# A fp32 transformer layer on one core: the last weight transfers in parts, a branch and a spread moved, and one quarter of the residual added by the array

## The chip, the cores and the metric

The kernel runs on one core of one Trainium2 chip. The metric is the device time of one execution, in microseconds (us). The engines of a core run their own instruction streams and wait for each other by semaphores: TensorE (PE) multiplies, VectorE (DVE) and ScalarE (ACT) do elementwise work, SyncE (SP) issues most transfers, GpSimd (POOL) makes constants.

## What is computed

One layer on 256 tokens of width 1024, all in float32: a mixer (dilated sliding attention and an mLSTM, with an output projection, added to x) gives x1, and a mixture of 32 experts, 4 for each token, gives what is added to x1.

```python
h = rmsnorm(x, norm1_g)
...
x = x + jnp.einsum('bse,ed->bsd', mixed, w_out[l])        # x1
x = x + moe_ffn(rmsnorm(x, norm2_g[l]), w_router[l], ...)

# moe_ffn, for the tokens tok of one expert e
gu = jnp.dot(xb, w_gate_up[e]) + b_gate_up[e]             # 1024 x 2048
gate = jnp.minimum(gu[:, :D_FF], SWIGLU_LIMIT)
up = jnp.clip(gu[:, D_FF:], -SWIGLU_LIMIT, SWIGLU_LIMIT)
act = gate * jax.nn.sigmoid(SWIGLU_ALPHA * gate) * (up + 1.0)
return jnp.dot(act, w_down[e]) + b_down[e]                # 1024 x 1024
```

## The kernel before

**Weights.** Every expert has 12 MB of weights: its gate and up matrix as 4 pieces of 2 MB (256 rows each, gate pieces in what follows) and its down matrix as 2 pieces of 2 MB (512 rows each, down pieces). A ring of 12 pieces in SBUF holds them. SP issues one transfer for each piece in the order of `LOAD_ORDER`: expert after expert, but at the end the four gate pieces of expert 30, the four of expert 31, the two down pieces of 30, and the two of 31. Before each, SP waits until PE has used what stood in that place of the ring (`gu_used`, `d_used`). One partition takes 16 KB of a piece. Only the very last piece comes as two transfers of 1 MB, the second one on the semaphore `ld_last`.

**Slots.** An expert works on 64 slots (CAP). PE gathers its tokens from x1 (`xres`) by a product with a 0/1 matrix (`pick`), turns them, multiplies them with the gate pieces into banks 0 and 1, and DVE and ACT make the activation `up_c` of them. PE turns that (`turn_act`), multiplies with the down pieces into bank 6 (`down`, ACT copies the result to `y_sb`, L787), and adds y to the tokens by a product with the turned slots (`spread`, L1509) into four banks of PSUM that stay open over all experts: `ACC`, one for each half of 128 tokens (t) and half of the width (c). `y_sb` has room for one expert, so the spread of an expert must be through before ACT copies the next one's y.

**Order on PE.** For each expert: the bias (L1413), the gate pieces (L1548), the slots' transposes (L1559), the spread of the expert before (L1509), the gathering for the next (L1475), `turn_act` (L1568), `turn_rows` (L1486) and the down pieces (L1584). Experts 1 to 28 run in a hardware loop of two (its branch is L1632); expert 0, expert 29 and the last two are written out. In `last_two` the gate pieces of 31 come ahead of the down pieces of 30, and the spread of 30 stands between the two down pieces of 31.

**Overflow.** If an expert has more than 64 tokens, rounds over all experts follow in a branch. DVE sets `flag` early; each engine loads it and compares (`overflow`, L384). In this data the flag is 0 and the branch jumps over the rounds' code. On PE this stands behind the last down products (L1643), and the last spread behind it.

**End.** DVE adds x1 to each of the four banks (L1136), SP stores each quarter of the output, 256 KB, when its sum is there (L542), and waits for all four.

The first part of the kernel, the mixer, takes some 150 us; nothing in it changes but semaphores that are merged.

## Time and profile before

| | |
|---|---|
| median of 3 runs | 1058.16 us (1057.73 to 1058.27) |
| profiled execution, its own time | 1057.47 us |
| its span, first to last instruction | 1055.7 us |
| mean granted TensorE clock | 1.000 |
| PE busy | 1035.1 us, 98% of the span |
| DVE, ACT busy | 198.9 us, 141.8 us |
| read from HBM | 423.31 MB, 402 GB/s over the span |

The profiled execution took 1.8 us more than its span, which is what lies around the program, and 0.7 us less than the median of the runs. PE counts as busy while matmuls overlap in it, so 98% doesn't say that it is at its peak. A 512-column float32 product stands in the profile as two MATMUL rows (two passes); those of 64 columns of weights run two at a time beside each other, so that the 16 rows of a 2 MB piece take 3.6 us. What bounds a stretch is read from what ended the idle time ahead of it, in brackets.

### The profile page before, as it was taken

How to read it: one execution, taken by the hardware profiler on the slowest of the kernel's cores; microseconds unless marked ns; L12 is line 12 of the kernel's file. 1: busy time of each engine (PE TensorE's matmuls, PEld its weight loads, DVE VectorE, ACT ScalarE, POOL GpSimd, SP SyncE). 2: the span in 40 equal slices, each digit the busy share in tenths (PEclk: the TensorE clock that was granted, in tenths of full speed). 3: DMA queues.
4: the chain of work that ended last, by engine and by line, in shares of the span. 5: the costliest groups of instructions: out<-in, count | busy, mean ns of one | idle time of the engine just before them, and what ended most of it. 6: DMA issues, size and time to landing. Idle time of an engine off the chain costs nothing.

```text
span 1055.7 us, 11898 instructions
## 1 busy us (share of the span) xinstructions
PE 1035.1 (98%) x4771; PEld 385.3 (37%) x4771; DVE 198.9 (19%) x502; ACT 141.8 (13%) x297; POOL 5.5 (1%) x23
## 2 busy tenths in 40 slices
PE   9999999999999999999999999999999999999997
PEld 5655543333333333333333333333333333233332
DVE  2162232111111111111111111111111111101111
ACT  2144431101111110010011111111111011001101
POOL 1000000000000000000000000000000000000000
PEclk9999999999999999999999999999999999999999
DMA  9964699999999999999999999999999999999996
GB/s 336 366 231 160 264 372 398 430 427 429 430 427 429 428 428 428 428 429 428 428 428 428 428 428 430 428 429 428 429 428 428 429 429 429 428 428 429 427 428 253
DMA packets 40875, 424.63 MB, mean 402 GB/s; under 512 B 6384, under 2 KB 7448, under 8 KB 15640
## 3 DMA queue, kind: packets, MB, share of 16 engines
q1 hardware_dynamic: 40840, 424.37, 95.9%
q8 instruction: 13, 0.21, 0.1%
q14 instruction: 6, 0.05, 0.0%
q10 hardware_dynamic: 16, 0.00, 0.0%
HBM read 423.31 MB, written 1.05 MB: 402 GB/s over the span
## 4 chain that ended last, share of the span: by engine, by line
PE 79%; DMA 14%; SPq 6%; issue 0%; DVE 0%; another core or an unknown queue 0%; ACT 0%; POOL 0%; DVEq 0%; POOLq 0%
PE bank L1548 33%; PE bank L1584 17%; DMA ring<-in_w_gate_up 14%; PE bank L1166 7%; PE bank L1509 4%; PE bank L1475 4%; SPq L392 4%; PE bank L1360 3%; PE bank L1413 2%; PE bank L1486 2%; PE bank L1568 2%; SPq L401 1%; PE bank L1202 1%; PE bank L1559 1%; PE bank L1144 0%
## 5 line engine op out<-in xcount | busy, mean ns | idle before, releaser
L1548 PE MATMUL bank<-ring,xe_t 128*64 128x512 f32 x2048 | 450.0, 594 | 10.3 <-DMA ring<-in_w_gate_up 9.8
L1548 PEld LDWEIGHTS bank<-ring,xe_t 128*64 128x64 f32 x2048 | 142.8, 137 | 314.0 <-issue 289.3
L1584 PE MATMUL bank<-ring,late 128*64 128x512 f32 x992 | 219.9, 595 | 0.6 <-DMA ring<-in_w_down 0.6
L1584 PEld LDWEIGHTS bank<-ring,late 128*64 128x64 f32 x992 | 68.8, 137 | 127.6 <-issue 124.0
L1085 DVE TENSOR_SCALAR gate_c<-bank 128x512 f32<-128x512 f32 x32 | 22.1, 692 | 439.4 <-PE bank L1548 439.4
L771 ACT ACTIVATE s_sb<-bank 128x256 f32<-128x256 f32 x32 | 12.3, 383 | 460.3 <-PE bank L1559 460.3
L1166 PE MATMUL bank<-ring 128*128 128x512 f32 x160 | 72.0, 596 | 0.5 <-issue 0.5
L1509 PE MATMUL bank<-late,s_sb 64*128 64x512 f32 x256 | 63.6, 615 | 0.7 <-ACT late L787 0.7
L1475 PE MATMUL bank<-xres,pick 128*64 128x512 f32 x248 | 60.0, 605 | 0.0
L787 ACT ACTIVATE late<-bank 128x512 f32<-128x512 f32 x32 | 19.1, 597 | 229.2 <-PE bank L1584 229.2
L1083 DVE COPY row_of<-fold 128x64 f32 x31 | 6.0, 195 | 195.1 <-PE bank L1413 195.1
L1166 PEld LDWEIGHTS bank<-ring 128*128 128x128 f32 x160 | 29.1, 190 | 31.6 <-issue 31.3
L1067 DVE TENSOR_TENSOR xe_t<-bank,g_run 128x512 f32<-128x512 f32 (+1 forms) x33 | 22.2, 675 | 87.5 <-PE bank L1486 87.4
L1413 PE MATMUL bank<-bgu,row_of 32*64 32x512 f32 x256 | 34.8, 613 | 0.0
L1509 PEld LDWEIGHTS bank<-late,s_sb 64*128 64x128 f32 x256 | 22.0, 186 | 22.5 <-issue 20.9
L1475 PEld LDWEIGHTS bank<-xres,pick 128*64 128x64 f32 x248 | 15.0, 136 | 41.2 <-issue 41.2
L760 ACT ACTIVATE late<-bank 128x512 f32<-128x512 f32 x31 | 18.5, 597 | 85.9 <-PE bank L1475 85.9
L1360 PE MATMUL bank<-ring 128*128 128x512 f32 x64 | 28.3, 592 | 0.0
L1568 PEld LDWEIGHTS bank<-ident,up_c 128*128 128x128 f32 x128 | 17.9, 210 | 26.0 <-issue 25.1
L1568 PE MATMUL bank<-ident,up_c 128*128 128x128 f32 x128 | 24.0, 310 | 0.0
L1486 PE MATMUL bank<-ident,late 128*128 128x128 f32 x124 | 23.1, 309 | 0.6
L1089 DVE SCALAR_TENSOR_TENSOR up_c<-up_c,gate_c 128x512 f32<-128x512 f32 x32 | 22.2, 692 | 1.2
(207 smaller groups left out, 420.4 us busy)
## 6 DMA issues: line engine op xcount, KB each, us to landing
ring<-in_w_gate_up SPq DMA_DIRECT2D x126, 2048.0 KB, 35.7
ring<-in_w_down SPq DMA_DIRECT2D x62, 2048.0 KB, 33.9
ring<-in_w_in SPq DMA_DIRECT2D x5, 2048.0 KB, 15.0
ring<-in_w_out SPq DMA_DIRECT2D x2, 2048.0 KB, 10.4
ring<-in_w_gate_up SPq DMA_DIRECT2D x4, 1024.0 KB, 8.0
ring<-in_w_down SPq DMA_DIRECT2D x4, 1024.0 KB, 25.7
ring<-in_attn_bias SPq DMA_DIRECT2D x1, 1536.0 KB, 18.1
xres<-in_x SPq DMA_DIRECT2D x2, 512.0 KB, 4.8
```

The lines of the kernel that those rows point to most:

```text
L392: sp.dma_start(gu_half(s), w_gate_up[0, e, h * RUN * P:(h + 1) * RUN * P, :].rearrange("(p j) n -> p j n", j=RUN))\
L1067: return dve.tensor_tensor(xe_t.rearrange("p (c b) n -> p c b n", c=2)[:, :, lo:hi, :], bank[7][:, :].rearrange("p (b c n) -> p c b n", b= ...
L1089: dve.scalar_tensor_tensor(out=up_c, in0=up_c, scalar=1.0, in1=gate_c, op0=ALU.add, op1=ALU.mult).then_inc(act_half, 1)
L1166: mm = pe.matmul(dst[:, :], ht[:, k, t * P:(t + 1) * P], win[:, b % WINS, k, :], start=(k == 0), stop=(k == KD - 1))
L1360: mm = pe.matmul(bank[ACC[2 * t + c]][:, :], mix_t[:, k, t * P:(t + 1) * P], wout[k // 4][:, k % 4, c * BANK:(c + 1) * BANK], start=(k == ...
L1413: mm = pe.matmul(bank[h][c * CAP:(c + 1) * CAP, :], row_of[rows, :], bgu[rows, :], start=True, stop=False, skip_group_check=True)
L1475: mm = pe.matmul(bank[7][c * CAP:(c + 1) * CAP, :], pick[:, t, :], xres[:, t, c * BANK:(c + 1) * BANK], start=(t == 0), stop=(t == T - 1), ...
L1486: mm = pe.transpose(bank[7][:, b * P:(b + 1) * P], runs[:, b // RUN, b % RUN, :], ident[:, :])
L1509: mm = pe.matmul(bank[ACC[2 * t + c]][:, :], s_sb[c * CAP:(c + 1) * CAP, u, t * P:(t + 1) * P], y_sb[c * CAP:(c + 1) * CAP, :], start=Fals ...
L1548: mm = pe.matmul(bank[h][c * CAP:(c + 1) * CAP, :], xe_t[:, k, :], w[:, k % RUN, at:at + BANK], start=False, stop=(k == KD - 1), skip_grou ...
L1568: mm = pe.transpose(dst[:, j * P:(j + 1) * P], act_runs[:, j, :], ident[:, :])
L1584: mm = pe.matmul(dst[c * CAP:(c + 1) * CAP, :], turned[:, at:at + CAP], w[:, k % DRUN, c * BANK:(c + 1) * BANK], start=(k == 0), stop=(k = ...
```

## The change

It does six things.

1. The fourth gate piece of experts 30 and 31 comes in two transfers of 1 MB (one of its two rows per partition each), the first down piece of 30 and 31 in two of 1 MB, and the second down piece of both in three, of 1 MB, 512 KB and 512 KB. PE waits for each part by a semaphore of its own (`ld_gate_end`, `ld_end`) just ahead of the products that read it. `ld_last` goes.
2. Expert 30's spread moves from between the two down pieces of 31 to right behind 30's own down products.
3. `last_two` is cut into `last_gates` and `last_downs`, and PE's load of the flag and its branch move between the two. The down products and the last spread now stand twice: in the branch's overflow arm, and in the usual arm, an Else, which stands last in the program.
4. `add_residual`: once, behind the loop and ahead of expert 29, PE adds the quarter t=1, c=1 of x1 to its bank by a product with the identity.
5. DVE adds x1 to three quarters and SP stores those. The fourth is copied from its bank by ACT, which then issues its store on its own queue, both behind ACT's own overflow branch.
6. Semaphores are merged, with the same waits in effect: `x_ms` and `f_log` into `act_step`, `pos_ready` into `dve_step`, `picked_t0` into `picked`.

```diff
+END_PARTS = {(NE - 2, 0): (0, 2), (NE - 2, 1): (0, 2, 3), (NE - 1, 0): (0, 2), (NE - 1, 1): (0, 2, 3)}
...
-        ld_last = sem("ld_last")
+        ld_gate_end = {n: sem(f"ld_gate_end_{n}") for n in (NE - 2, NE - 1)}
+        ld_end = {(n, c, lo): sem(f"ld_end_{n}_{c}_{lo}") for (n, c), cuts in END_PARTS.items() for lo in cuts[1:]}
...
-            def load_d(e, c, s, halves=False):
+            def load_d(e, c, s, cuts=(0,)):
                 rows = w_down[0, e, c * DRUN * P:(c + 1) * DRUN * P, :].rearrange("(p j) n -> p j n", j=DRUN)
...
+                for lo, hi in zip(cuts, cuts[1:] + (DRUN,)):
+                    loaded = ld_end[e, c, lo] if lo else ld_piece[s]
+                    sp.dma_start(down_piece(s)[:, lo:hi, :], rows[:, lo:hi, :]).then_inc(loaded, 16)
...
-                next_gu(base, 0, NE - 2)
-                next_gu(base, 0, NE - 1)
+                for n in (NE - 2, NE - 1):
+                    next_gu(base, 0, n, GUN - 1)
+                    s = piece_of(n, GUN - 1)
...
+                    sp.dma_start(gu_half(s)[:, 0:1, :], rows[:, 0:1, :]).then_inc(ld_piece[s], 16)
+                    sp.dma_start(gu_half(s)[:, 1:RUN, :], rows[:, 1:RUN, :]).then_inc(ld_gate_end[n], 16)
...
# ACT, at its end
+            t = T - 1
+            act.wait_ge(acc_final, 2 * T)
+            act.activation(xres[:, t, BANK:2 * BANK], bank[ACC[2 * t + 1]][:, :], ACT.Copy).then_inc(x_copied, 1)
+            act.wait_ge(x_copied, 1)
+            act.dma_start(out[0, t * P:(t + 1) * P, BANK:2 * BANK], xres[:, t, BANK:2 * BANK]).then_inc(stored, 16)
...
# PE
+            def add_residual():
+
+                t = T - 1
+                pe.matmul(bank[ACC[2 * t + 1]][:, :], ident[:, :], xres[:, t, BANK:2 * BANK], start=False, stop=False,
+                          skip_group_check=True)
...
+                    if n >= NE - 2 and k == KD - 1:
+                        pe.wait_ge(ld_gate_end[n], 16 * round_no + 16)
...
-                    if n == NE - 1 and k == KD - DRUN // 2:
-                        pe.wait_ge(ld_last, 16 * round_no + 16)
+                    elif (n, k // DRUN, k % DRUN) in ld_end:
+                        pe.wait_ge(ld_end[n, k // DRUN, k % DRUN], 16 * round_no + 16)
...
+            def last_downs(base, round_no):
+
+                n = NE - 2
+                now = base + n
                 down(now, 0, n, round_no, act_t, ks=range(DRUN))
                 turn_act(now + 1, bank[7])
                 down(now, 0, n, round_no, act_t, ks=range(DRUN, KD))
-                down(now + 1, 0, n + 1, round_no, last_t, bank[0], range(DRUN))
                 for t in range(T):
                     spread(now, tint(n), t)
-                down(now + 1, 0, n + 1, round_no, last_t, bank[0], range(DRUN, KD))
+                down(now + 1, 0, n + 1, round_no, last_t, bank[0])
...
             more = overflow(pe)
             with pe.If(more > 0):
+                last_downs(0, 0)
                 with pe.Fori(1, ROUNDS) as r:
...
                     experts(r * NE, r)
+                    last_downs(r * NE, r)
                 pe.wait_ge(bank6_read, ROUNDS * NE + 1)
-            for t in range(T):
-                spread(NE - 1, tint(NE - 1), t, acc_final)
+                last_spread()
+            with pe.Else():
+                last_downs(0, 0)
+                last_spread()
```

Names in the rows that follow: `ring` holds the weights, `pickg` the slots, `up_c` the activation, `late` is `act_t` or `y_sb`, `xe_t` is also the turned activation of expert 31. First, PE's stream from the slots' transposes of expert 31 on, before:

```order
L1559 MATMUL bank<-ident,pickg 128x128 [waits pickg_ready]
L1559 MATMUL bank<-ident,pickg 128x128
L1584 MATMUL bank<-ring,late 64x512 [waits ld_piece8,act_t_ready]
L1584 MATMUL bank<-ring,late 64x512 x7
L1568 MATMUL bank<-ident,up_c 128x128 [waits slots_ready,act_ready]
```

and in the changed kernel:

```order
L1574 MATMUL bank<-ident,pickg 128x128 [waits pickg_ready]
L1574 MATMUL bank<-ident,pickg 128x128
L383 TENSOR_LOAD flag [waits flag_ready]
L383 ISA x2
L1669 COMPARE_AND_BRANCH
L1599 MATMUL bank<-ring,late 64x512 [waits ld_piece8,act_t_ready]
L1599 MATMUL bank<-ring,late 64x512 x3
L1599 MATMUL bank<-ring,late 64x512 [waits ld_end_30_0_2]
L1599 MATMUL bank<-ring,late 64x512 x3
L1583 MATMUL bank<-ident,up_c 128x128 [waits slots_ready,act_ready]
```

The load of the flag and the branch have come in between the transposes and the first down product; behind the branch the overflow arm stands first (shown here, its first rows are those of the usual arm), and the usual arm last, so that the branch is taken and goes past all of the overflow arm. Second, PE's stream from the second down piece of 30 to the branch, before:

```order
L1584 MATMUL bank<-ring,late 64x512 [waits ld_piece9,act_t_ready]
L1584 MATMUL bank<-ring,late 64x512 x7
L1584 MATMUL bank<-ring,xe_t 64x512 [waits ld_piece10,act_t_ready]
L1584 MATMUL bank<-ring,xe_t 64x512 x7
L1509 MATMUL bank<-late,s_sb 128x512 [waits bank6_read]
...
L1584 MATMUL bank<-ring,xe_t 64x512 [waits ld_piece11,act_t_ready]
L1584 MATMUL bank<-ring,xe_t 64x512 x3
L1584 MATMUL bank<-ring,xe_t 64x512 [waits ld_last]
L1584 MATMUL bank<-ring,xe_t 64x512 x3
L384 TENSOR_LOAD flag [waits flag_ready]
L384 ISA x2
L1643 COMPARE_AND_BRANCH
```

and now:

```order
L1599 MATMUL bank<-ring,late 64x512 [waits ld_piece9,act_t_ready]
L1599 MATMUL bank<-ring,late 64x512 x3
L1599 MATMUL bank<-ring,late 64x512 [waits ld_end_30_1_2]
L1599 MATMUL bank<-ring,late 64x512
L1599 MATMUL bank<-ring,late 64x512 [waits ld_end_30_1_3]
L1599 MATMUL bank<-ring,late 64x512
L1522 MATMUL bank<-late,s_sb 128x512 [waits bank6_read]
...
L1599 MATMUL bank<-ring,xe_t 64x512 [waits ld_piece10,act_t_ready]
L1599 MATMUL bank<-ring,xe_t 64x512 x3
L1599 MATMUL bank<-ring,xe_t 64x512 [waits ld_end_31_0_2]
```

The spread of 30 now waits for ACT's copy (`bank6_read`) with no product of 31 ahead of it, and each piece has a wait for each part. Third, SP's transfers from the gate pieces of 31 on, before:

```order
L392 DMA ring<-in_w_gate_up 128x4096 [waits gu_used] x2
L401 DMA ring<-in_w_down 128x4096 [waits gu_used] x2
L401 DMA ring<-in_w_down 128x4096 [waits d_used]
L398 DMA ring<-in_w_down 128x2048 [waits d_used]
L399 DMA ring<-in_w_down 128x2048
```

and now:

```order
L525 DMA ring<-in_w_gate_up 128x2048 [waits gu_used]
L526 DMA ring<-in_w_gate_up 128x2048
L398 DMA ring<-in_w_down 128x2048 [waits gu_used]
...
L398 DMA ring<-in_w_down 128x2048 [waits d_used]
L398 DMA ring<-in_w_down 128x1024 x2
```

From 30's fourth gate piece on, which is split the same way, nine pieces are left; they took 10 transfers before and take 17 now.

## Rows read from the trace of the kernel before

**Rows 1.** The page: slices of the span, and a queue (packets, MB, share).

```profile
DMA  9964699999999999999999999999999999999996
GB/s 336 366 231 160 264 372 398 430 427 429 430 427 429 428 428 428 428 429 428 428 428 428 428 428 430 428 429 428 429 428 428 429 429 429 428 428 429 427 428 253
...
q8 instruction: 13, 0.21, 0.1%
```

**Rows 2.** Stretches of the end: us, busy by engine, PEclk, DMA share, GB/s.

```profile
953.00:1005.00 52.00, 49.24 (x232) 16.18 (x228) 6.36 (x16) 4.58 (x8) 0.00 (x0) 1.00 1.01 428
1005.00:1029.60 24.60, 24.50 (x116) 8.46 (x116) 4.21 (x8) 2.19 (x4) 0.00 (x0) 1.00 1.01 427
1029.60:1049.00 19.40, 17.14 (x76) 6.10 (x76) 2.34 (x4) 2.47 (x5) 0.00 (x0) 1.00 0.67 284
```

**Rows 3.** PE in order of time: start, us, line, names [idle before <-releaser].

```profile
970.83 3.65 PE L1548 MATMUL bank<-ring,xe_t 128*64 128x512 f32 x16 [0.17 <-DMA ring<-in_w_gate_up]
...
1000.18 3.65 PE L1548 MATMUL bank<-ring,xe_t 128*64 128x512 f32 x16 [0.15 <-DMA ring<-in_w_gate_up]
1005.07 3.65 PE L1548 MATMUL bank<-ring,xe_t 128*64 128x512 f32 x16 [1.24 <-DMA ring<-in_w_gate_up]
...
1015.26 13.95 PE L1548 MATMUL bank<-ring,xe_t 128*64 128x512 f32 x64
1029.15 0.44 PE L1559 MATMUL bank<-ident,pickg 128*128 128x128 f32 x2
1029.63 3.65 PE L1584 MATMUL bank<-ring,late 128*64 128x512 f32 x16
1033.22 0.75 PE L1568 MATMUL bank<-ident,up_c 128*128 128x128 f32 x4
1034.52 3.65 PE L1584 MATMUL bank<-ring,late 128*64 128x512 f32 x16 [0.56 <-DMA ring<-in_w_down]
1039.42 3.65 PE L1584 MATMUL bank<-ring,xe_t 128*64 128x512 f32 x16 [1.24 <-DMA ring<-in_w_down]
1043.01 1.99 PE L1509 MATMUL bank<-late,s_sb 64*128 64x512 f32 x8
1044.92 3.65 PE L1584 MATMUL bank<-ring,xe_t 128*64 128x512 f32 x16
1049.27 1.99 PE L1509 MATMUL bank<-late,s_sb 64*128 64x512 f32 x8 [0.70 <-ACT late L787]
```

**Rows 4.** SP's transfers: L399's landing, and SP's issues in order of time.

```profile
DMA to landing us min/median/max: 43.5/43.5/43.5
...
647.25 3.76 SPq L401 DMA_DIRECT2D ring<-in_w_down  x2
...
940.81 39.11 SPq L392 DMA_DIRECT2D ring<-in_w_gate_up  x8
979.96 12.80 SPq L401 DMA_DIRECT2D ring<-in_w_down  x3
992.80 7.90 SPq L398 DMA_DIRECT2D ring<-in_w_down  x1
1000.74 4.25 SPq L399 DMA_DIRECT2D ring<-in_w_down  x1
```

**Rows 5.** Flag load and branches on the sequencers: xcount, ns min/median/max, start.

```profile
L384 PEldq TENSOR_LOAD <-flag x1: 481/481/481, 1044.9 to 1044.9; - x1
L1643 PEldq COMPARE_BRANCH  x1: 3385/3385/3385, 1045.8 to 1045.8; - x1
L1632 PEldq COMPARE_BRANCH  x14: 83/215/252, 233.5 to 958.3; - x14
L818 ACTq COMPARE_BRANCH  x1: 54/54/54, 1049.4 to 1049.4; - x1
```

**Rows 6.** DMA from 1045 to 1050, in 40 slices of 0.125 us, and by queue.

```profile
DMA  0000000000000040000000000000000000000005
GB/s 0 0 0 0 0 0 0 0 0 0 0 0 0 0 131 0 0 0 0 0 0 0 0 0 0 0 0 0 0 0 0 0 0 0 0 0 0 0 0 131
q8 instruction: 2, 0.03, 2.6%
```

**Rows 7.** ACT's copies and the last sums and stores, in order of time.

```profile
1038.22 0.60 ACT L787 ACTIVATE late<-bank 128x512 f32<-128x512 f32 x1 [3.62 <-PE bank L1584]
...
1048.62 0.60 ACT L787 ACTIVATE late<-bank 128x512 f32<-128x512 f32 x1 [9.81 <-PE bank L1584]
...
1050.43 2.48 DVE L1136 TENSOR_TENSOR xres<-bank,xres 128x512 f32<-128x512 f32 x4 [18.35 <-PE bank L1509]
1051.15 2.12 SPq L542 DMA_DIRECT2D out<-xres  x4
```

**Rows 8.** Stretches of the last 3 us, columns as in rows 2.

```profile
1051.00:1052.00 1.00, 0.26 (x2) 0.00 (x0) 1.00 (x3) 0.00 (x0) 0.00 (x0) 1.00 0.00 0
1052.00:1052.50 0.50, 0.00 (x0) 0.00 (x0) 0.50 (x2) 0.00 (x0) 0.00 (x0) 1.00 0.97 360
...
1054.00:1054.50 0.50, 0.00 (x0) 0.00 (x0) 0.00 (x0) 0.00 (x0) 0.00 (x0) 1.00 1.02 381
```

**Rows 9.** The page, products of 128 full columns.

```profile
L1166 PE MATMUL bank<-ring 128*128 128x512 f32 x160 | 72.0, 596 | 0.5 <-issue 0.5
```

More of the change, by code:

```diff
@@ L259, in layer_kernel @@
         act_step = sem("act_step")
-        x_ms = sem("x_ms")
         x_rs = sem("x_rs")
@@ L474, in free_of, with next_gu @@
                 return gu_used, GUN * base + GUN * m + was + 1
-            def next_gu(base, far, n):
-                for h in range(GUN):
+            def next_gu(base, far, n, pieces=GUN):
+                for h in range(pieces):
                     used, count = free_of(base, n, h)
@@ L487, in next_d @@
                     sp.wait_ge(used, count + (GUN if used is gu_used else DN) * far)
-                    load_d(far + n, c, piece_of(n, GUN + c), n == NE - 1 and c == DN - 1)
+                    load_d(far + n, c, piece_of(n, GUN + c), END_PARTS.get((n, c), (0,)))
             def third(base, round_no):
@@ L538, in _ @@
                     weights(base, r)
-            for t in range(T):
-                for c in range(2):
-                    sp.wait_ge(x_final, 2 * t + c + 1)
-                    sp.dma_start(out[0, t * P:(t + 1) * P, c * BANK:(c + 1) * BANK],
-                                 xres[:, t, c * BANK:(c + 1) * BANK]).then_inc(stored, 16)
+            for g in range(2 * T - 1):
+                t, c = g // 2, g % 2
+                sp.wait_ge(x_final, g + 1)
+                sp.dma_start(out[0, t * P:(t + 1) * P, c * BANK:(c + 1) * BANK],
+                             xres[:, t, c * BANK:(c + 1) * BANK]).then_inc(stored, 16)
             sp.wait_ge(stored, 16 * 2 * T)
@@ L624, in _ @@
             act.activation(rows_l, rows_l, ACT.Exp).then_inc(act_step, 1)
-            act.wait_ge(act_step, 5)
-            act.activation(rows_l, rows_l, ACT.Ln, bias=1.0).then_inc(f_log, 1)
+            act.wait_ge(act_step, 2 * T + 3)
+            act.activation(rows_l, rows_l, ACT.Ln, bias=1.0).then_inc(act_step, 1)
             act.wait_ge(conv_ready, HM)
@@ L1131, in _ @@
                     experts(base)
-            for t in range(T):
-                for c in range(2):
-                    dve.wait_ge(acc_final, 2 * t + c + 1)
-                    xs = xres[:, t, c * BANK:(c + 1) * BANK]
-                    dve.tensor_tensor(xs, bank[ACC[2 * t + c]][:, :], xs, ALU.add).then_inc(x_final, 1)
+            for g in range(2 * T - 1):
+                dve.wait_ge(acc_final, g + 1)
+                xs = xres[:, g // 2, (g % 2) * BANK:(g % 2 + 1) * BANK]
+                dve.tensor_tensor(xs, bank[ACC[g]][:, :], xs, ALU.add).then_inc(x_final, 1)
         @block.tensor
@@ L1641, in _, with last_spread @@
             experts(0, 0, start_sum)
+            def last_spread():
+                for t in range(T):
+                    spread(NE - 1, tint(NE - 1), t, acc_final)
             more = overflow(pe)
             with pe.If(more > 0):
+                last_downs(0, 0)
                 with pe.Fori(1, ROUNDS) as r:
@@ L1649, in _ @@
                     experts(r * NE, r)
+                    last_downs(r * NE, r)
                 pe.wait_ge(bank6_read, ROUNDS * NE + 1)
-            for t in range(T):
-                spread(NE - 1, tint(NE - 1), t, acc_final)
+                last_spread()
+            with pe.Else():
+                last_downs(0, 0)
+                last_spread()
 _INS = ['x', 'norm1_g', 'w_in', 'q_norm_g', 'k_norm_g', 'conv_w', 'conv_b', 'w_mq', 'w_mk', 'b_igate', 'b_fgate',
```

48 lines of the change are left out of this document (23 added, 25 removed).

## The prediction

> **What bounds the kernel now.** I read the page's slices first. From the eighth slice on the DMA engines are full at some 428 GB/s to within a slice of the end [rows 1], and every edit here but the merged semaphores lies in the last 100 us. The weights' stream is fixed, so its end is too: the last transfer is issued at 1000.74 us and lands 43.5 us later, at 1044.2 [rows 4]. What can be won is what PE has still to do around and behind that. So I went to PE in order of time [rows 3] and looked in the brackets for waits that the transfers end. There are three large ones behind the loop's last expert: 1.24 us at 1005.07 (fourth gate piece of 30), 0.56 at 1034.52 (second down piece of 30), 1.24 at 1039.42 (first down piece of 31). Landings are 4.89 us apart (1000.18 to 1005.07, and 1034.52 to 1039.42 nearly the same), a piece takes PE 3.6. From 1005.07 to 1034 nothing waits: 24.50 of 24.60 us are busy [rows 2], so here an earlier start of PE is kept, until the next landing. Behind the last products come ACT's copy of y (1048.62, 0.60), the last spread at 1049.27, and the sums and stores [rows 3, 7].
>
> **The parts of the pieces.** With the fourth gate piece of 30 in halves, the first half is there 2.4 us before 1005.0, so PE goes straight on at 1003.83 (1000.18 plus 3.65) and needs the second half 1.8 us later, at 1005.6, when it has landed. The wait of 1.24 goes, and the 24 us behind it move up by 1.24: gate products of 31 end at 1027.9 and the slots' transposes at 1028.3 instead of 1029.5. The later gate pieces allow it: at 4.89 us apart behind 1005.0 the fourth of 31 lands at 1024.6 and PE comes to it at 1024.5 (15.26 less 1.24, plus three quarters of 13.9), which the halves cover. The first down piece of 30 lands in whole at 1029.5, its first half at 1027.1, so it isn't waited for.
>
> **The chain from there.** From the start of 30's down products to the last spread, each step from rows 3 and 7: first piece 3.59 (1029.63 to 1033.22), turn_act 0.75, second piece until ACT's copy 3.70 (1034.52 to 1038.22), copy and start of the spread 0.65 (1048.62 to 1049.27), spread of 30 1.91 (1043.01 to 1044.92), first piece of 31 3.59, second until the copy 3.70, copy 0.65. Sum 18.54 us. The waits for transfers are gone if the parts are early enough: first half of the second piece of 30 lands at 1032.0, last quarter at 1034.4; the pieces of 31 at 1039.3 and 1044.2, the halves 2.4 us before. A start at 1028.4 needs them at 1032.7, 1035.4, 1038.9 (half), 1040.7 and 1045.2 (last quarter), so all are in time, by little. The new place of the spread costs its 0.65 us of waiting for ACT, which one piece of products hid before (and before that the 1.24 us of waiting stood there); that is in the sum. Had nothing else changed, the last spread would start at 1028.36 + 18.54 = 1046.90, 2.37 us before 1049.27.
>
> **The branch.** Before, PE's sequencer loads the flag at 1044.9 and branches at 1045.8; the branch takes 3385 ns [rows 5]. The loop's branches take 83 to 252 ns [rows 5], and beside the long one an instruction fetch runs on a queue of its own, at 1046.8, 1 us behind the branch's start [rows 6]. So I read it as the cost of going on at code that isn't there, and the changed kernel jumps past as much code. It ends at 1049.2, when ACT's copy also ends (1049.22) [rows 7]: before, it is just hidden. It is so by the products that the sequencer had handed over in advance: at 1044.92 sixteen rows of PE were still to run [rows 3]. Moved ahead of 30's down products, it has the transposes (2 rows, 0.4 us) and some 12 to 14 rows of gate products ahead of it, 3.0 to 3.4 us. From the flag's load to the next instruction it is 0.9 + 3.39 + 0.07 = 4.3 us (1044.94 to 1049.27 has room for no more). PE stands still for 4.3 less 3.2 = 1.1 us. The transfers now run at full rate beside the fetch, where before they had ended: a 16 KB packet of weights takes 0.61 us (4.89 us over the 8 that each of 16 engines has of a piece), and the two fetches of rows 6 took 2.6% of 5 us times 16 engines, 1.04 each. I add 0.4 for a packet ahead and a slower fetch. So 1.5 us, with both ends: nothing, if the branch's 3385 ns were mostly a wait for PE's queue to drain, and 3.4 if nothing hides it. 30's down products then start at 1028.3 + 1.5 = 1029.8, after 1029.63 before: the 1.24 us won at the gate piece are spent here.
>
> The Trainium skill (Runtime: NRT & Kernel Launch, Instruction fetch mechanics) says that a taken branch whose target lies outside the fetched window stalls until the target page is fetched by DMA, and this trace's fetch inside the 3385 ns agrees. It speaks against this change: the branch leaves a place where ACT's copy covered it. By the figure of another page (Advanced Engine Details and Errata, Control Flow Timing), 108 ns for a compare and branch, nothing would be lost and the gain were the full 2.4 us; the row decides for the first.
>
> **What costs nothing.** The added product of x1 has 128 columns, two rows of 0.45 us [rows 9], 0.9 in all. It stands ahead of expert 29, where PE waits 0.17 and, soon after, 1.23 us for gate pieces (970.83 is the first) [rows 3]; the later wait takes it. Were this not so it would cost 0.9. SP issues 17 transfers for 10. In a free queue an issue is short (two in 3.76 us with their waits, at 647 us), in a full one it takes what the queue drains, 4.89 us each (8 in 39.11) [rows 4]. Counted so, the queue holds about nine transfers, so that with parts the last is let in when the ninth or tenth ahead of it lands, near 1025, still 17 us before its turn; the DMA engines never run dry. A fixed 4.9 us for each would let the last in at 940.8 + 3 x 4.9 (the three gate pieces ahead) + 17 x 4.9 = 1039, still ahead of its turn. Parts of 8 KB a partition landed at the same rate as whole pieces; for 4 KB no row stands, at most some 0.2 us.
>
> **The end.** DVE's four sums start 0.6 us apart, so taking the fourth away looks like 0.6 us. It isn't: from 1052.0 on the stores fill the DMA engines, at 360 to 381 GB/s [rows 8], and 1 MB at that rate takes 2.8 us however early the last one is issued. The first store's issue (1051.15) sets it, and that isn't changed. I take 0, with 0.6 as the other end. ACT's branch took 54 ns at 1049.4 [rows 5], and its copy is wanted 2 us later.
>
> **Sum.** Last spread at 1029.8 + 18.54 = 1048.35 for 1049.27: 0.9 us earlier. Profiled execution 1057.47 to 1056.6; the runs' median lies 0.7 above that execution, so 1058.16 goes to 1057.2.
>
> **Rivals.** (a) Gain small as above, 1057.2: chance 0.64. It covers stalls from 0.5 to 2.4 us.
> (b) The branch is hidden or short. For: it ended within 0.05 us of ACT's copy, and PE's queue had just emptied, so it may not have been a pure fetch. Against: the fetch beside it. Then the gain is 2.4, with up to 0.6 more from the end: 1055.2 to 1055.8. Chance 0.24.
> (c) The fetch waits behind weights. It needs a turn on a DMA engine whose queue is full, which before it never did with PE waiting. If it stands behind the 8 packets of one transfer, 4.9 us, PE's stall is 1.1 + 4.9 = 6.0 and the last spread starts at 1028.3 + 6.0 + 18.5 = 1052.8: 3.6 us slower, 1061.7. It decides for slower from a stall of 2.4 us, and beyond the noise from 4.5. A fetch of two pages one after the other is the same case. Against: the same queue made 13 fetches over the span, most of them beside full transfers [rows 1], and PE shows next to no gap from 1005 to 1029.6 [rows 2]; but those may have been ahead of need. Chance 0.12, half of it beyond 1060.3.
> The same arbitration is told by the Trainium skill (DMA: Bandwidth & Descriptors, Queues, rings and completion order): a DMA engine drains a whole packet of 9 to 17 descriptors of one queue before it turns to the next. No row here shows how long a fetch stood in line.
>
> **Numbers.** A measurement of this kernel tells about 0.2%, 2.1 us, from no change. Faster than that needs a gain of 2.1 and so a stall below 0.3 us or a gain at the end: 0.24. Slower: 0.07. Else the same, 0.69. The range runs from the low end of (b), 1055.3, to a stall of 3.4 us with 0.2 of slow parts, 1059.3.
>
> **What would show it.** The wait at 1005 gone and PE's transposes of 31 at 1027.9; an idle of 1 to 2 us ahead of 30's first down product, with a long COMPARE_BRANCH beside it; waits of 0.7 for ACT ahead of both last spreads and none for a transfer behind 1005; the last spread at 1048.3; stores at full rate for 2.8 us. I am wrong if the branch row is short, if it is above 5 us, or if the stores end less than 2.8 us behind the first.

## The result, and the profile after

The changed kernel takes 1061.37 us, median of 8 runs, against 1057.95 for the kernel before (8 runs on the same chip): ratio 1.0026, 95% interval 1.0017 to 1.0036 (the ratios here are taken over the runs and are not exactly the quotients of the medians). It is 3.4 us slower; 1057.2 was predicted, with a range up to 1059.3. Seven of the eight runs lie between 1058.05 and 1062.05. The eighth took 2146.91 us at full clock; I can't explain it, it didn't come back in ten further runs, and the ratio leaves it out.

| | before | after |
|---|---|---|
| profiled execution, its own time | 1057.47 | 1061.84 |
| its span | 1055.7 | 1060.1 |
| mean granted TensorE clock | 1.000 | 0.996 |
| PE busy | 1035.1 | 1038.5 |
| last spread's start | 1049.27 | 1053.71 |
| from there to the span's end | 6.4 | 6.4 |

All of the loss is there by the start of the last spread, 4.44 us later. The page after, to be laid beside [rows 1]:

```profile
span 1060.1 us, 11922 instructions
...
PEclk9999999999999999999999999999999999999998
...
GB/s 338 366 225 159 268 372 399 427 428 429 427 430 430 427 428 428 429 428 429 429 427 429 429 428 429 429 428 429 429 428 429 429 428 428 430 426 429 426 419 196
...
q8 instruction: 13, 0.21, 0.1%
```

The stream of weights is as before; new is an 8 in the last slice of PEclk. Next, PE in order of time, the changed kernel's rows for [rows 3] (start, us, names, [idle before <-releaser]):

```profile
993.57 14.32 PE L1563 MATMUL bank<-ring,xe_t 128*64 128x512 f32 x64
...
1014.44 13.95 PE L1563 MATMUL bank<-ring,xe_t 128*64 128x512 f32 x64
1028.32 0.44 PE L1574 MATMUL bank<-ident,pickg 128*128 128x128 f32 x2
1032.64 6.41 PE L1599 MATMUL bank<-ring,late 128*64 128x512 f32 x16 [3.88 <-issue]
1038.98 0.75 PE L1583 MATMUL bank<-ident,up_c 128*128 128x128 f32 x4
1039.65 3.65 PE L1599 MATMUL bank<-ring,late 128*64 128x512 f32 x16
1044.01 1.99 PE L1522 MATMUL bank<-late,s_sb 64*128 64x512 f32 x8 [0.70 <-ACT late L790]
1045.92 7.09 PE L1599 MATMUL bank<-ring,xe_t 128*64 128x512 f32 x32
1053.71 1.99 PE L1522 MATMUL bank<-late,s_sb 64*128 64x512 f32 x8 [0.70 <-ACT late L790]
```

No row waits for a transfer: the 64 products of 30's gate pieces (993.57) run through, where 1.24 us of waiting stood, and so do all down pieces. In place of three waits of 3.04 us stand an idle of 3.88 us that ends by "issue", with no releaser, and a first down piece of 6.41 us for 3.65. The sequencer's own rows beside it (the flag's load, the branch, and the last down part's transfer with its time to landing):

```profile
L383 PEldq TENSOR_LOAD <-flag x1: 492/492/492, 1025.5 to 1025.5; - x1
```
```profile
L1669 PEldq COMPARE_BRANCH  x1: 6132/6132/6132, 1026.3 to 1026.3; - x1
```
```profile
L398 SPq DMA_DIRECT2D ring<-in_w_down x1: 3196/3196/3196, 1022.6 to 1022.6; - x1
...
DMA to landing us min/median/max: 22.7/22.7/22.7
```

The branch takes 6132 ns for 3385 [rows 5]. Stretches of this time (us, busy by engine, PEclk, DMA share, GB/s), the rows for [rows 2]:

```profile
1026.30:1028.70 2.40, 2.40 (x12) 0.63 (x8) 0.26 (x1) 0.00 (x0) 0.00 (x0) 1.00 1.02 423
1028.70:1031.40 2.70, 0.06 (x1) 0.00 (x0) 2.41 (x4) 0.90 (x2) 0.00 (x0) 1.00 0.99 399
1031.40:1032.60 1.20, 0.00 (x0) 0.00 (x0) 0.00 (x0) 0.00 (x0) 0.00 (x0) 0.50 1.02 410
1032.60:1038.20 5.60, 5.56 (x14) 1.91 (x16) 0.00 (x0) 0.00 (x0) 0.00 (x0) 0.50 1.03 423
1038.20:1053.70 15.50, 14.11 (x64) 4.51 (x60) 0.00 (x0) 1.79 (x3) 0.00 (x0) 1.00 0.35 142
```

2.6 us after PE's last work (1028.76) the granted clock fell from 1.00 to 0.50, which is 1.2 of 2.4 GHz, and it stayed there for the first 5.6 us of products. One packet of instructions went over its queue in these six microseconds; in the trace's records of single packets it starts 3.63 us behind the branch's start, where in the kernel before, with the transfers over, it was 1.04. The packet itself took 1.07 us for 0.93, and from its end to the branch's end it is 1.4 us in both. So nearly all of the longer branch is time before the fetch starts.

What let the flag's load and the branch begin is, by the times, a landing. The second half of 31's fourth gate piece was issued at 984.9 and landed 40.5 us later, at 1025.4, and the flag's load starts 0.1 us behind that:

```profile
L526 SPq DMA_DIRECT2D ring<-in_w_gate_up x1: 4237/4237/4237, 984.9 to 984.9; - x1
...
DMA to landing us min/median/max: 40.5/40.5/40.5
```

The end, for [rows 7]:

```profile
1054.87 1.89 DVE L1143 TENSOR_TENSOR xres<-bank,xres 128x512 f32<-128x512 f32 x3 [23.62 <-PE bank L1522]
1055.59 1.53 SPq L545 DMA_DIRECT2D out<-xres  x3
1055.77 0.60 ACT L827 ACTIVATE xres<-bank 128x512 f32<-128x512 f32 x1 [2.11 <-PE bank L1522]
1056.39 0.38 ACTq L829 DMA_DIRECT2D out<-xres  x1
```

Three sums instead of four, and the fourth store is issued by ACT at 1056.39, yet the distance from last spread to end is unchanged.

### The profile page after: what moved, and what is told of

Read it like the earlier page. It is cut to its first block, busy times and chain, and to the rows that moved or that the text cites. A ratio compares the mean times of both kernels' runs of the same rounds, so it can differ in the third digit from the quotient of the medians.

```text
span 1060.1 us, 11922 instructions
## 1 busy us (share of the span) xinstructions
PE 1038.5 (98%) x4773; PEld 386.3 (36%) x4773; DVE 198.3 (19%) x501; ACT 142.4 (13%) x298; POOL 5.5 (1%) x23
## 4 chain that ended last, share of the span: by engine, by line
PE 78%; SPq 10%; DMA 9%; issue 1%; DVE 0%; ACT 0%; POOL 0%; DVEq 0%; another core or an unknown queue 0%; POOLq 0%
PE bank L1563 32%; PE bank L1599 17%; DMA ring<-in_w_gate_up 9%; SPq L391 7%; PE bank L1173 7%; PE bank L1522 4%; PE bank L1482 4%; SPq L398 3%; PE bank L1367 3%; PE bank L1420 2%; PE bank L1493 2%; PE bank L1583 2%; PE bank L1209 1%; PE bank L1574 1%; PE bank L1151 0%
## 5 line engine op out<-in xcount | busy, mean ns | idle before, releaser
L1599 PE MATMUL bank<-ring,late 128*64 128x512 f32 x992 | 222.7, 601 | 3.9 <-issue 3.9
```

The costliest lines, as they stand in the source:

```text
L1599: mm = pe.matmul(dst[c * CAP:(c + 1) * CAP, :], turned[:, at:at + CAP], w[:, k % DRUN, c * BANK:(c + 1) * BANK], start=(k == 0), stop=(k = ...
```

## The experiments

The kernels are numbered here; in the expectations, e1 is kernel 1, e7 kernel 2, e2 kernel 4, e10 kernel 12.

My theory: the branch fetches code that isn't there, the fetch stands in line behind the weights' packets (6.13 us for 3.39), and PE, standing still for so long, loses its clock as well. Rivals: the fetch is long for another reason (the larger code behind it); the clock falls because of the fetch and not because of the pause; or the parts, the spread's place or the end carry the loss. All medians are of 6 to 11 runs beside the kernel before on the same chip. Where a branch's time is given as min/median/max it is in ns.

**1. The usual arm first.** The changed kernel with its arms exchanged, so that the branch falls through to the code behind it.

```diff
-            with pe.If(more > 0):
+            with pe.If(more < 1):
+                last_downs(0, 0)
+                last_spread()
+            with pe.Else():
                 last_downs(0, 0)
...
-            with pe.Else():
-                last_downs(0, 0)
-                last_spread()
```

> The changed kernel with the two arms of PE's branch exchanged: the usual arm stands right behind the branch (If more < 1) and the overflow arm last. Theory A (the loss is the taken branch: PE stands still while its target code is fetched behind the weights, and its clock then falls): the branch isn't taken, its row is short (0.05 to 0.3 us), 30's down products start within 0.1 us of the transposes' end, no stretch shows the lower clock, and the last spread starts at 1046.9: 1055.6 us, 2.4 faster than before. Theory B (the loss comes of the split transfers or of the spread's new place): it stays at 1058 us or above, whatever the branch does.

1057.24 against 1058.04: 0.9991 (0.9982 to 1.0000). The branches and PE in order of time:

```profile
L1669 PEldq COMPARE_BRANCH  x2: 83/1836/3588, 1026.1 to 1047.0; - x2
```
```profile
1028.40 3.65 PE L1599 MATMUL bank<-ring,late 128*64 128x512 f32 x16
...
1037.05 1.99 PE L1522 MATMUL bank<-late,s_sb 64*128 64x512 f32 x8 [0.69 <-ACT late L790]
1038.96 7.30 PE L1599 MATMUL bank<-ring,xe_t 128*64 128x512 f32 x32
1046.96 1.99 PE L1522 MATMUL bank<-late,s_sb 64*128 64x512 f32 x8 [0.70 <-ACT late L790]
```

The branch takes 83 ns, there is no idle and no fall of the clock, and the last spread starts at 1046.96, 0.06 from the 1046.90 that the prediction had without a stall, 2.31 us earlier than before. So the whole difference of 6.75 us at the last spread between the changed kernel and this one (1053.71 to 1046.96) comes with the jump. But the total gains only 0.8, since the end now comes 8.3 us behind the last spread, for 6.4. Stretches of the end of this kernel, and the time to landing of SP's stores (before: 2.0/2.2/2.3):

```profile
1049.70:1052.60 2.90, 0.00 (x0) 0.00 (x0) 0.31 (x1) 0.00 (x0) 0.00 (x0) 1.00 0.97 358
1052.60:1053.80 1.20, 0.00 (x0) 0.00 (x0) 0.00 (x0) 0.00 (x0) 0.00 (x0) 0.72 0.06 17
```
```profile
DMA to landing us min/median/max: 2.1/2.2/4.8
```

The stores flow for 2.9 us as before, then a few packets are left. In the packet records an instruction fetch runs from 1052.88 to 1053.84, and the last two store packets start behind it, one after the other (1053.82 and 1054.04); the records don't say which DMA engine a packet ran on. The jump out of the first arm (3588 ns from 1047.0) is what this kernel has there and the changed kernel doesn't.

**2, 3. Code put between the arms.** If that late fetch were the next page behind the jump's target, more code in the overflow arm might shift it.

```diff
             with pe.Else():
+                for _ in range(32):
+                    pe.matmul(bank[1][:, 0:P], ones[:, :], ident[:, :], start=True, stop=True)
                 last_downs(0, 0)
```

> e1 with 32 products put into the overflow arm that never runs, so that the code behind it moves by 128 instructions at most, half of a 16 KB fetch. If e1's end is late because PE's last fetch (1052.88, beside the stores) holds two store packets back, it depends on where the code ends: the fetch may fall away or come at another time, and the end then comes 6.4 us behind the last spread as in the kernel before, 1055.5 us. If the late end has another cause: as e1, 1057.2.

> As e7 with 48 products, three quarters of a fetch. Either the end is 1055.5 us (no fetch beside the stores) or 1057.2 (as e1). If the jump's target comes to lie just ahead of the end of what is fetched, a second fetch can hold PE's end, but nothing waits for PE by then.

1057.06 (0.9993, 0.9984 to 1.0002) with 32 such products and 1057.03 (0.9991, 0.9982 to 1.0000) with 48. The fetch still comes at 1052.87 and 1052.91, and the end is as late as in 1. The padding does nothing; that the fetch holds the stores is read from the order of packets, not shown. What is shown is that the late end goes with the jump out of the arm: kernel 9 has it too and ends 8.3 us behind its last spread, while the changed kernel and kernel 13, with the same stores and no jump near the end, end 6.4 us behind it.

**4. The branch at its old place.** The changed kernel with the down products ahead of the branch again, and nothing else undone.

```diff
+            last_downs(0, 0)
             more = overflow(pe)
             with pe.If(more > 0):
-                last_downs(0, 0)
...
-                last_spread()
-            with pe.Else():
-                last_downs(0, 0)
-                last_spread()
+            last_spread()
```

> The changed kernel with the branch back where it was, behind the last down products; all else as changed. Theory A: no stall ahead of 30's down products. The flag's load comes some 3.6 us before the products end, near 1042.6, the branch near 1043.5. The weights are nearly through then, so it takes 3.4 to 4.5 us and ends at 1046.9 to 1048.0, beside or up to 1 us behind ACT's copy: 1055.7 to 1056.7 us. If it is as long as in the changed kernel (6.1) it ends at 1049.6: 1058.3. Theory B: 1058 us or above with waits elsewhere.

1058.56 against 1058.04: 1.0004 (0.9995 to 1.0013). Flag, branch, and the last spread:

```profile
L383 PEldq TENSOR_LOAD <-flag x1: 482/482/482, 1045.1 to 1045.1; - x1
```
```profile
L1670 PEldq COMPARE_BRANCH  x1: 3383/3383/3383, 1046.0 to 1046.0; - x1
```
```profile
1049.42 3.40 PE L1522 MATMUL bank<-late,s_sb 64*128 64x512 f32 x8 [3.12 <-issue]
```

The products end at 1046.3, 2.3 us earlier than before, and nothing is won: I expected the flag's load at 1042.6, but the sequencer stands at its wait for the last part, which lands at about 1045.05, and only then comes to the flag. From there it is 0.9 and 3.38 us, whatever PE has left to do. The 1058.3 of the expectation is near by luck: it stood there for a branch of 6.1 us. In the kernel before it was not the landing that set the branch: its last piece landed at 1044.2 (1000.74 plus 43.5) [rows 4], and the flag's load came 0.7 us later, just as PE began its last 16 rows (1044.92). Kernel 11, in the same order, has the same two distances (0.73 us behind the landing, 0.02 behind the start of those rows); what holds the load there isn't shown. With PE earlier, the landing is what is left. And the spread behind the pause ran at half clock (3.40 us for 1.99).

**5, 6. Two small moves on 4:** the flag loaded ahead of 30's down products, so that only the branch waits for the last landing; and 30's spread back between 31's down pieces.

```diff
# 5
-            last_downs(0, 0)
             more = overflow(pe)
+            last_downs(0, 0)
# 6
+                down(now + 1, 0, n + 1, round_no, last_t, bank[0], range(DRUN))
                 for t in range(T):
                     spread(now, tint(n), t)
-                down(now + 1, 0, n + 1, round_no, last_t, bank[0])
+                down(now + 1, 0, n + 1, round_no, last_t, bank[0], range(DRUN, KD))
```

> e2 (branch at the end) with the flag loaded ahead of the down products, the branch alone left at the end. If the branch in e2 starts when the wait for the last landing (1045.05) lets PE's sequencer through: it starts 0.87 us earlier, at 1045.1, ends at 1048.5, and the last spread starts there: 1057.7 us, 0.9 faster than e2. If it starts when so many rows are left in PE's queue (16): it would start at 1042.6 already and end at 1046.0 to 1047, 1055.7 us.

> e2 with 30's spread back between the two down pieces of 31: the transfers in parts and the tail, in the old order. The last landing plus 4.3 us of flag and branch sets the last spread (1049.4) as in e2, so the spread's place makes no difference: 1058.5 us. If the place of the spread matters: 0.3 to 0.7 apart from e2.

The first: 1057.82 against 1057.94, 0.9997 (0.9988 to 1.0006), 0.74 us below 4, as expected of a branch that waits for the landing. It starts there:

```profile
L1670 PEldq COMPARE_BRANCH  x1: 3682/3682/3682, 1045.2 to 1045.2; - x1
```

The second: 1058.28, 1.0002 (0.9993 to 1.0011), its last spread at 1049.43. With the branch there, the spread's place makes no difference. In the old order PE does wait for parts (1.33 and 0.46 us ahead of the halves of 31's first down piece).

**7. The branch alone**, in the kernel before, whole pieces kept.

```diff
             more = overflow(pe)
             with pe.If(more > 0):
+                last_downs(0, 0)
...
+                last_spread()
+            with pe.Else():
+                last_downs(0, 0)
+                last_spread()
```

> The kernel before with the branch alone moved ahead of 30's down products, the usual arm last. Theory A: 30's down products start 3.5 to 4 us later (1033.5), their first 16 rows take some 6.4 us at the lower clock for 3.6, and the two waits for transfers behind them (0.56 and 1.24) go: last spread near 1054, 1062.5 us, 4.5 slower than before. If the clock doesn't fall: 1060. Theory B: 1058 to 1059.

1058.14 against 1058.04: 1.0003 (0.9994 to 1.0012), 4 us less than expected. The branch, the piece behind it, and that piece's stretch:

```profile
L1653 PEldq COMPARE_BRANCH  x1: 6412/6412/6412, 1025.8 to 1025.8; - x1
```
```profile
1032.43 5.35 PE L1584 MATMUL bank<-ring,late 128*64 128x512 f32 x16 [2.64 <-issue]
```
```profile
1032.40:1037.70 5.30, 5.27 (x16) 1.76 (x16) 0.00 (x0) 0.00 (x0) 0.00 (x0) 0.68 0.97 410
```

The long branch is there without any of the other edits, and so is the slow piece. But PE still had its waits of 0.56 and 1.24 for whole down pieces behind it [rows 3], and in the profile they are gone, so 1.8 us of the loss were paid out of them. The 2.64 of idle and 1.70 of slower products make 4.3, and the last spread is 2.4 later than before, at 1051.67. The eleven runs fall apart into eight of 1057.6 to 1058.2 at a mean clock of 0.999 or 1.000 and three of 1059.4 to 1060.2 at 0.998. So the fall of the clock seems to come in some executions only, and to cost about 2 us; only the profiled one, of the three, shows it in rows. PE stands still for less than in the changed kernel although the branch is longer, because the flag's load, at 1025.0, comes 4.8 us ahead of the transposes' end, for 3.3 there: the landing of 31's last gate piece lets the sequencer through in both (1024.8 and 1025.4), and the changed kernel's PE is a microsecond earlier.

**8. The branch with no weights in flight.** The changed kernel without the transfers of the last four down pieces, nor PE's waits for them (the last down products multiply with what stands in the ring).

```diff
-                next_d(base, 0, NE - 2)
-                next_d(base, 0, NE - 1)
...
-                    if k % DRUN == 0:
+                    if k % DRUN == 0 and n < NE - 2:
...
-                    elif (n, k // DRUN, k % DRUN) in ld_end:
-                        pe.wait_ge(ld_end[n, k // DRUN, k % DRUN], 16 * round_no + 16)
```

> The changed kernel without the loads of the last four down pieces (both of 30 and both of 31) and without PE's waits for them; the products read what stands in the ring. Its branch is where it is in the changed kernel, but the weights end near 1025. If the fetch stood in line behind weights: the branch row falls from 6.1 us towards 3.4 to 4, PE stands still ahead of 30's down products for about 1.1 to 1.7 us instead of 3.9, and the last spread starts at 1048 to 1049. If the branch was longer for its place in PE's stream (PE's queue, the transposes) or for its code: it stays at 6 us.

1056.05 against 1057.98: 0.9984 (0.9973 to 0.9994), all runs at a clock of 1.0.

```profile
L1665 PEldq COMPARE_BRANCH  x1: 3432/3432/3432, 1025.6 to 1025.6; - x1
```
```profile
1029.13 3.65 PE L1595 MATMUL bank<-ring,late 128*64 128x512 f32 x16 [1.03 <-issue]
```

The same jump at the same place over the same code takes 3432 ns and PE stands for 1.03 us, as the prediction reckoned (1.1) before its extra. Its fetch starts 1.0 us behind the branch's start again. So transfers in flight add 2.7 us ahead of the fetch, and this, not the code's size, is what was missing.

**9. A pause without a fetch.** Kernel 1 (near branch), in which PE waits for two more operations of DVE ahead of the down products.

```diff
+            for i in range(2):
+                settle()
+                step(dve.tensor_scalar(gate_c, gate_c, 1.0, None, ALU.mult))
+            settle()
+            dve.engine_nop().then_inc(paused, 1)
...
             with pe.If(more < 1):
+                pe.wait_ge(paused, 1)
                 last_downs(0, 0)
```

> The kernel of e1 (no branch taken, no fetch) with a pause put ahead of 30's down products: PE waits there for two extra 0.7 us operations of DVE behind its last activation, until about 1032.8, as long as the changed kernel stood for its branch. If PE's clock falls for PE standing still: a stretch at granted clock 0.5 follows, the first down piece takes about 6.4 us for 3.65, the last spread starts near 1053.9, 1061 to 1062 us and slower than before by 3 to 4. If it fell for the fetch or the branch itself, or by chance: the clock stays at 1.0 and the last spread starts at 1032.8 + 18.5 = 1051.3, 1059 us.

1060.67 against 1057.98: 1.0029 (1.0017 to 1.0041), 3.4 us over kernel 1.

```profile
1031.75 3.65 PE L1605 MATMUL bank<-ring,late 128*64 128x512 f32 x16 [3.40 <-DVEq L1133]
```

In the profiled execution a pause of 3.40 us left the clock alone, and 3.4 us is no more than the pause itself. Of the six runs three, this one among them, took 1059.8 to 1060.2 at a mean of 0.999; the other three, at 0.998, 0.998 and 0.995, took 1061.1 to 1062.5. Kernel 1 has runs at 0.998 too, none at 0.995, so in one of these runs the clock fell, and probably in all three; no profile shows one of them. That a pause without a fetch can be enough is shown by the kernel before, at its end, where PE is through at 1051.3, only stores are in flight and no instruction fetch runs:

```profile
1051.30:1054.80 3.50, 0.00 (x0) 0.00 (x0) 1.62 (x3) 0.00 (x0) 0.00 (x0) 1.00 0.80 299
1054.90:1055.60 0.70, 0.00 (x0) 0.00 (x0) 0.00 (x0) 0.00 (x0) 0.00 (x0) 0.50 0.00 0
```

**10. The changed kernel again.**

> The changed kernel once more, beside the others of this call. Its branch stands 6.1 us under full transfers; PE stands still for 3 to 4 us. Executions in which the clock then falls: 1060.8 to 1062; in which it doesn't: 1058 to 1059. If its slower time was of the first chip: within 0.1% of before.

1061.44 against 1057.94: 1.0029 (1.0019 to 1.0038). Branch 6212 ns, idle 3.97, first piece 6.49. Seven of ten runs at a clock of 0.996 took 1061.1 to 1062.0, three at 0.998 took 1060.1 to 1060.4.

**11. The end's copy and store alone**, with the added product, in the kernel before (the parts 4 and 5 of the change).

> The kernel before with only the x1 quarter added by PE, three sums on DVE, and the fourth copied and stored by ACT. If the stores fill the DMA engines at the end, as I read the slices: no change, 1058.0 within 0.1. If the fourth sum on DVE were what the end waits for: 0.6 faster, 1057.4. If the added product of 0.9 us isn't covered ahead of expert 29: up to 0.9 slower.

1057.91 against 1058.04: 0.9998 (0.9989 to 1.0007). Nothing, as predicted.

**12, 13. The branch where its stall has cover.** If a stall of PE is harmless as long as PE waits for transfers later, the branch belongs early. Once behind expert 0, once behind 8 of the loop's 14 rounds; the rest of PE's stream then stands in both arms.

```diff
# 13; 12 is the same without the first laps
-            experts(0, 0, start_sum)
+            expert(0, 0, 0, 0, start_sum)
+            laps(0, 0, 0, 8)
...
             more = overflow(pe)
             with pe.If(more > 0):
+                laps(0, 0, 8, LAPS)
+                rest(0, 0, start_sum)
                 last_downs(0, 0)
...
             with pe.Else():
+                laps(0, 0, 8, LAPS)
+                rest(0, 0, start_sum)
                 last_downs(0, 0)
```

> The changed kernel with PE's flag load and branch behind expert 0, near 175 us, and the whole rest of PE's stream in both arms, so that the usual arm ends the program and no taken branch stands near the end. If the stall of 4 to 6 us there is hidden, since the transfers have 20 us of work queued and bound the whole: the last spread at 1047.0, no fetch beside the stores, the end 6.4 us behind it, 1055.2 us, 2.8 faster than before. If a stall of PE so early delays the transfers: that much later, up to 1059. If the late end of e1 wasn't the fetch: 1057.1.

1058.61 against 1057.94: 1.0002 (0.9993 to 1.0011). Ten microseconds at its branch (6212 ns from 179.4):

```profile
185.00:190.00 5.00, 4.08 (x14) 1.07 (x16) 0.20 (x1) 0.00 (x0) 0.00 (x0) 0.53 1.03 437
190.00:195.00 5.00, 5.00 (x20) 1.46 (x18) 0.00 (x0) 0.00 (x0) 0.00 (x0) 0.79 0.34 95
```

Here the ring wasn't yet a buffer: PE freed pieces late, and the transfers dropped to 95 GB/s for 5 us. The last spread is at 1051.96. A stall with cover on PE's side still starved the stream. The profiled execution (1060.06) is the slowest of the eleven, beside another of the same time; the two fastest, 1056.55 and 1056.9, ran at a mean clock of 1.000, so the fall of the clock seems to be a large part of the loss here.

> As e10, but the branch stands behind 8 of the loop's 14 rounds, near 618 us, where transfers land some 38 us after their issue, and each arm has the other 6 rounds and the rest. Theory: the stall of PE (6.2 us of branch less its queue, perhaps with a stretch at the lower clock) is hidden, the last landing stays near 1045.1, the last spread starts at 1047.0, and no fetch stands beside the stores, so that the end comes 6.4 us later, at 1053.4: 1055.2 us. If the late end of e1 had another cause than the fetch: 1057.1. If the stall delays the transfers here too: the last landing moves by that, up to 1059.

1056.32 against 1058.12: 0.9985 (0.9976 to 0.9994). This one is faster than both kernels, by 0.15% of the kernel before. Its branch, the stretch with it, the last spread, and its stores' times to landing:

```profile
L1678 PEldq COMPARE_BRANCH  x1: 6457/6457/6457, 619.6 to 619.6; - x1
```
```profile
620.00:630.00 10.00, 6.55 (x35) 1.85 (x33) 0.20 (x1) 0.60 (x1) 0.00 (x0) 1.00 1.00 424
```
```profile
1047.72 1.99 PE L1522 MATMUL bank<-late,s_sb 64*128 64x512 f32 x8 [0.70 <-ACT late L790]
```
```profile
DMA to landing us min/median/max: 2.1/2.1/2.9
```

PE stands for 3.45 us, the transfers go on at 424 GB/s, and nearly all of the 3.45 us is made good by later waits. The last spread is 1.55 us earlier than before, and the end again 6.4 us behind it. The spread is 0.7 us later than expected, since the last landing was at 1045.8 and not at 1045.1.

**14. That place of the branch alone**, in the kernel before.

> The kernel before with the branch alone put there, behind 8 of 14 rounds; no parts, no other edit. In the kernel before the branch was just hidden beside ACT's copy, so the last spread stays at 1049.3 and the time at 1058.0, within 0.2. If the branch at the end cost the kernel before anything, it is gained here; if the two copies of the loop cost something (fetches, the second loop's start), it is lost here.

1058.94 against 1058.12: 1.0009 (1.0000 to 1.0018); last landing 1045.7, last spread 1050.80, the waits of 0.55 and 1.25 as before. Its branch is another far one under full transfers (6417 ns), and the whole stream is later behind it. Set against the kernel before, the landings in the trace of kernel 14 are level at 565 us, 0.4 us late at 628, 0.6 at 663, and 1.5 from 972 on, where PE waits 1.00 us for the third gate piece of 29, for 0.17 before [rows 3]:

```profile
972.36 3.65 PE L1548 MATMUL bank<-ring,xe_t 128*64 128x512 f32 x16 [1.00 <-DMA ring<-in_w_gate_up]
```

In kernel 13 the landings are 0.6 us late at 565 and 1.1 at 1000; in kernel 1 and in the changed kernel the distance (0.3 and 0.6) stays as it is between these two times. So this place of the branch does delay the transfers, by 0.5 us in the one profile and 1.5 in the other. An instruction fetch of PE starts at 967.25, beside the late piece of kernel 14; whether it is the cause isn't shown.

## Why the prediction was wrong

**The parts: right.** The wait at 1005 is gone, no row waits for a transfer behind it. The slots' transposes were to start at 1027.9 and end at 1028.3; they start at 1028.32 and end at 1028.76, since the whole stream of this execution is late: its landings are 0.6 us behind those of the kernel before from 902 us on. In kernel 1 they end at 1028.40. Kernel 1 measured parts and spread's place together at 2.31 us against 2.37.

**The chain: right, by kernel 1,** 18.56 us (1028.40 to 1046.96) for 18.54. In the changed kernel it is 21.07.

**The branch: the step that failed** is "I add 0.4 for a packet ahead and a slower fetch". The size of the cover (3.3 us from the flag's load to the transposes' end) and the 1.1 us without a line were right (kernel 8: 1.03). The time in line was 2.7 us instead of 0.4 (branches of 6.13, 6.21, 6.41, 6.21, 6.46 and 6.42 us beside full transfers; 3.38 to 3.80 with them over or left out), and the packet records put it ahead of the fetch, whose own length hardly changes. Rival (c) had this mechanism with 4.9 us at a chance of 0.12, the forecast with 0.4: the truth lay between, 2.7. My argument against it, 13 fetches beside full transfers with no gap on PE, counted fetches that may have run ahead of need, as the sentence itself said; they carry no word on one that is needed. The page of the Trainium skill cited with (c) (DMA: Bandwidth & Descriptors, Queues, rings and completion order) has a DMA engine drain a packet of 9 to 17 descriptors of one queue before it turns to the next. The delay agrees in kind, and by this rule I should have given (c) more; the 2.6 us by which the fetch starts later are 4 of the 0.61 us packets of the trace, and the runs don't show which it stood behind.

That the cover came out right was in part luck. I took it from rows that the sequencer had handed over in advance; in the changed kernel and in kernels 1 to 3, 5 and 8 to 10 the flag's load starts 0.1 us behind the landing of 31's last gate part. The parts move PE forward and not this landing, so each microsecond won at the gate piece is one less of cover: it was 4.8 us in kernel 7 and 3.3 here.

**The clock: a term that was missing.** I priced a pause at its length. In the profiled execution it cost 2.76 us more, since 16 products took 6.41 us for 3.65. Together: start of the downs 1032.64 for 1029.8 (2.38 of longer stall; the other 0.46 is the transposes' later end), chain 21.07 for 18.54 (2.76 of clock, less 0.15 in the last 32 products, which run through, and 0.08 between 30's two pieces). 2.84 + 2.53 = 5.4 us at the last spread, 1053.71 for 1048.35. Of the 4.2 us between the medians (1061.37 for 1057.2), the line is about 2.4 and the clock most of the rest; the spread of runs at 1060.1 to 1062.0 fits a clock loss of different length in each.

**The cover: right in kind, wrong as a saving.** In the kernel before, the branch was hidden by the last 16 rows, as I read it. But kernel 4 shows the sequencer held at the wait for the last landing once PE is earlier. So the old place costs at least the landing plus 4.3 us, which any gain on PE runs into, and the parts without the branch's move give nothing (kernels 4 and 6). The change was right to see that the branch had to go; its new place had only 3.3 us of cover, and full DMA engines.

**What costs nothing, and the end: right.** Kernel 11 gives 0 for the added product, the copy and the store. SP's 17 transfers kept the engines full. The last one landed at 1045.3 (issued 1022.6, plus 22.7) for 1044.2; about 0.6 of that is there before the first part, so the parts cost some 0.5, where I said 0.2. The added product took 1.06 us for 0.9 (963.19 to 964.25) and was covered.

**Open:** what decides whether the clock falls; the one changed-kernel run at full clock that took 1058.05, 1.0 us less than the profiled execution would take without its 2.76 of clock (1059.1); what in the jump makes kernel 1's end late; what delays single landings in kernels 13 and 14; the run of 2146.91.

## What to carry to other kernels

Price a jump to code that isn't fetched by what the DMA engines do at that moment: 3.4 us when they are idle and 6.1 to 6.5 us beside full transfers here. The usual arm placed first costs 0.08, but the jump out of it is then the far one, and here the end came 1.9 us later with it. PE's sequencer held at a wait couldn't begin the flag load or branch behind it, so count as cover only what PE still has to run when that wait is over; put the branch where PE waits for transfers later and a deep ring keeps the transfers going (kernel 13, 1.8 us faster than before). When a change opens a pause of microseconds in PE, add what the clock may cost behind it.

## What the runs showed of the hardware that I had not expected

- The granted clock fell to 0.50 after 2.6 us without PE work, and came back 5.6 us into the products (changed kernel). In kernel 4 the spread behind 3.12 us of idle ran at 0.50, in kernel 5 that behind 2.54 us. In kernel 7 PE started again after 2.64 us at 1.00, and the clock fell 1.0 us into the products (mean of the piece 0.68); in kernel 14 it was 1.3 us into them, behind 3.41 us. Kernel 9 with 3.40 us and kernel 13 with 3.45 us, at the same place as kernel 14, show no fall in their profiles.
- Six far branches beside full transfers took 6.13 to 6.46 us, their fetches starting 3.6 to 4.0 us behind the branch's start; six with the transfers over or left out took 3.38 to 3.80, their fetches starting at 1.0.
- A wait for a landing on PE held its flag load too: in kernel 4 it came at 1045.1, at the landing, with 1.2 us of products still to run, and in the changed kernel 0.1 us behind the landing of the last gate part.
- In kernel 1 one instruction fetch of a single packet amid the stores goes with a store that lands after 4.8 us instead of 2.2.
